# Row maxima of two long attentions taken in parts of 512 keys, rows made by VectorE transposes, a third score bank and values four steps late

## The reference

```python
def gqa_attend(q, k, v):
    s = jnp.einsum('bqhgd,bkhd->bhgqk', q, k).astype(jnp.float32) * (GQA_HEAD_DIM ** -0.5)
    p = jax.nn.softmax(s, axis=-1).astype(v.dtype)
    return jnp.einsum('bhgqk,bkhd->bqhgd', p, v)

def mla_attend(q_nope, q_rope, k_nope, k_rope, v):
    s = (jnp.einsum('bqhd,bkhd->bhqk', q_nope, k_nope)
         + jnp.einsum('bqhr,bkr->bhqk', q_rope, k_rope)).astype(jnp.float32) * ((MLA_NOPE + MLA_ROPE) ** -0.5)
    p = jax.nn.softmax(s, axis=-1).astype(v.dtype)
    return jnp.einsum('bhqk,bkhd->bqhd', p, v)
```

## Time and profile before

| | us |
|---|---|
| median of 3 runs | 3588.08 (3584.24 to 3592.72) |
| the profiled execution's own time | 3586.85 |
| its span, first to last instruction | 3585.0 |
| PE busy in the span | 3351.6 (93%) |
| DVE, ACT, POOL busy | 2186.5 (61%), 1793.4 (50%), 1535.2 (43%) |
| GQA attention, first maxima to the end of its values | about 1819.6 to 2381 |
| MLA attention, the same | about 2917.9 to 3487 |

### The profile page before, as it was taken

The page is one execution under the profiler, slowest core; times in us unless marked ns, Lnnn a source line. Parts: engine busy times, 40 slices in busy tenths (PEclk is TensorE's granted clock), DMA queues, the critical chain, the costliest instruction groups (busy, mean ns, idle before and its releaser), DMA issues.

```text
span 3585.0 us, 47856 instructions
## 1 busy us (share of the span) xinstructions
PE 3351.6 (93%) x14934; PEld 2655.1 (74%) x14934; DVE 2186.5 (61%) x2655; ACT 1793.4 (50%) x3060; POOL 1535.2 (43%) x977
## 2 busy tenths in 40 slices
PE   7999999999999999799889999989888989999999
PEld 5777877778888887587777777767765667777767
DVE  6674877477575757447246666666558865555551
ACT  3343868242010101434158888861465657887870
POOL 3303444434444444510156666656210026666652
PEclk9999999999999999899999999999999989999999
DMA  2134232311212121123433443412254344332311
GB/s 99 53 117 119 75 77 81 119 41 66 75 59 88 55 86 35 58 102 115 124 89 66 102 85 76 103 64 89 97 197 149 118 118 111 65 82 53 76 42 71
DMA packets 196086, 313.52 MB, mean 87 GB/s; under 512 B 100928, under 2 KB 111680, under 8 KB 195968
## 3 DMA queue, kind: packets, MB, share of 16 engines
q1 hardware_dynamic: 195968, 312.01, 29.8%
HBM read 234.02 MB, written 77.92 MB: 87 GB/s over the span
## 4 chain that ended last, share of the span: by engine, by line
PE 68%; DVE 12%; issue 7%; ACT 6%; POOL 3%; DMA 2%; SPq 2%; DVEq 0%; ACTq 0%; POOLq 0%
PE PBX L281 10%; PE PBX L283 10%; PE PBX L282 10%; PE PMX L281 5%; PE PMX L282 5%; PE PMX L283 5%; PE PMX L1952 4%; PE PD L1993 2%; PE PD L1994 2%; PE PD L1995 2%; PE PD L856 2%; DVE gqa_m L2083 1%; PE PBX L1977 1%; PE PBX L1976 1%; PE PBX L1978 1%
## 5 line engine op out<-in xcount | busy, mean ns | idle before, releaser
L216 POOL TENSOR_TENSOR w_hi<-w_stage,zero 128x1024 fp32r<-128x1024 f32 (+2 forms) x123 | 229.1, 1863 | 1263.4 <-PE PBX L283 789.3
L2061 POOL TENSOR_TENSOR gqa_pl<-gqa_pf,gqa_ph 128x512 fp32r<-128x512 f32 (+1 forms) x288 | 370.9, 1305 | 186.3 <-ACT gqa_ph L2034 185.7
L2061 POOL TENSOR_TENSOR mla_pl<-mla_pf,mla_ph 128x512 fp32r<-128x512 f32 x256 | 351.8, 1383 | 206.9 <-ACT mla_ph L2034 202.7
L2083 DVE TENSOR_REDUCE gqa_m<-PMX 128x1 f32<-128x1280 f32 (+1 forms) x158 | 200.9, 1271 | 173.6 <-PE PMX L1952 172.7
L218 POOL TENSOR_TENSOR w_lo<-w_stage,w_hi 128x1024 fp32r<-128x1024 f32 (+2 forms) x123 | 299.9, 2438 | 9.7
L1678 ACT ACTIVATE conv_in<-PBX 128x512 f32<-128x512 f32 x66 | 39.6, 601 | 480.6 <-PE PBX L283 476.6
L2083 DVE TENSOR_REDUCE mla_m<-PMX 128x1 f32<-128x1280 f32 x126 | 187.3, 1487 | 89.5 <-PE PMX L1952 88.9
L2029 ACT ACTIVATE mla_pf<-PBX 128x512 f32<-128x512 f32 x320 | 190.1, 594 | 98.0 <-PE PBX L1978 88.1
L2029 ACT ACTIVATE gqa_pf<-PBX 128x512 f32<-128x512 f32 (+1 forms) x352 | 202.1, 574 | 52.8 <-PE PBX L1981 48.6
L2034 ACT ACTIVATE gqa_ph<-gqa_pf 128x512 fp32r<-128x512 f32 (+1 forms) x352 | 215.6, 612 | 13.8
L281 PE MATMUL PBX<-ffn_hi,w_hi 128*128 128x512 f32 x528 | 207.5, 393 | 8.5 <-DVE ffn_lo L653 8.5
(11 more groups left out here) (411 smaller groups left out, 9915.1 us busy)
## 6 DMA issues: line engine op xcount, KB each, us to landing
mod_w<-in_w_mod SPq DMA_DIRECT2D x48, 512.0 KB, 3.5
w_stage<-in_w_up SPq DMA_DIRECT2D x44, 512.0 KB, 3.4
w_stage<-in_w_go SPq DMA_DIRECT2D x24, 512.0 KB, 3.8
gqa_k<-kh_d SPq DMA_DIRECT2D x32, 320.0 KB, 4.9
gqa_q<-qh_d SPq DMA_DIRECT2D x32, 320.0 KB, 7.7
w_stage<-in_w_down SPq DMA_DIRECT2D x24, 384.0 KB, 3.0
qh_d<-heads_qh SPq DMA_DIRECT2D x32, 256.0 KB, 2.0
ql_d<-heads_ql SPq DMA_DIRECT2D x32, 256.0 KB, 2.3
```

The costliest lines, as they stand in the source:

```text
L216: pool.tensor_tensor(w_hi[s][:, 0:st.cols], w_stage[s][:, 0:st.cols], z, ALU.add).then_inc(w_hi_done, 1)
L2061: eng.tensor_tensor(self.PL[k % 4][:, 0:n], self.PF[k % 4][:, 0:n], self.PH[k % 4][:, 0:n].bitcast(F32), ALU.subtract).then_inc(self.lo_dv ...
L2083: dve.tensor_reduce(self.M[g % 2][:, t:t + 1], MX[:, 0:w], AX.X, ALU.max, negate=True)\
```

## The change

- Maxima are taken in **parts** of 512, 512 and 256 keys (`part_keys`): each part is one matmul and one reduction, and goes to one of two banks of PMX in turn. The parts of a tile are spread over two steps.
- The row is made on DVE alone (`row`): a small reduction over the parts with the sign turned, four 32-partition transposes and a copy. `diag`, `bcast` and ACT's `row` are gone.
- Scores have 3 banks in GQA and 4 in MLA, and `PF`, `PH`, `PL` rings of 6 and 5 in place of 4. `O` has a bank for each chunk.
- `LAG` is 4 in place of 3 for PE and ACT, and `LAG + 2` for DVE's `final`.
- The two half-width steps of the context chunk are one step, so a GQA head has 21 steps.
- The plan: the coming head's first maxima stand at step 11 (GQA; 12 before) and 10 (MLA, as before), and its second chunk's first tile is taken in the same head too.

```diff
-            LAG = 3
+            LAG = 4
...
-                self.S = [PB[0], PB[1]]
-                self.BC = PB[2]
-                self.O = [PD[0], PD[1]]
+                self.S = [PB[0], PB[1], PB[2]] + [PMX[:, 2 * C:3 * C]] * self.mla
+                self.NS, self.NP = len(self.S), len(self.PF)
+                self.O = [PD[0], PD[1], PMX[:, 2 * C:3 * C]][:len(chunks)]
+                self.MX = [PMX[:, 0:C], PMX[:, C:2 * C]]
...
-                    plan = [(2 * t, "max", (0, 1), t) for t in range(4)] + [(8, "bcast", (0, 1), 0)]
-                    plan += [(8 + 2 * t, "max", (0, 2), t) for t in range(2)] + [(12, "bcast", (0, 2), 0)]
-                    plan += [(12 + 2 * t, "max", (1, 0), t) for t in range(4)] + [(21, "bcast", (1, 0), 0)]
+                    plan = [u for t in range(1, 4) for u in tile((2 * t - 2, 2 * t - 1, 2 * t - 1), (0, 1), t)]
+                    plan += [(7 + t, (0, 2), t, 0) for t in range(2)]
+                    plan += [u for t in range(4) for u in tile((11 + 2 * t, 12 + 2 * t, 12 + 2 * t), (1, 0), t)]
+                    plan += tile((19, 20, 20), (1, 1), 0)
...
-                        sp.wait_ge(self.pv, i * self.SB + (CR_PV2 + self.SB // 2))
+                        sp.wait_ge(self.pv, i * self.SB + (self.NP + self.SB // 2))
...
-                    pe.wait_ge(self.exp, i * SB + (k - 2 + CR_E + 1))
+                    pe.wait_ge(self.exp, i * SB + (k + 1))
...
+                    for b in range(4):
+                        dve.transpose(blocks[:, :, b, :], NEG[32 * b:32 * b + 32, 0:m, :]).then_inc(self.turned, 1)
...
-                self.run(dve, step, lambda i, k: final(i, k) if self.steps[k][4] else None)
+                self.run(dve, step, lambda i, k: final(i, k) if self.steps[k][4] else None, lag=self.LAG + 2)
```

More of the change, by code:

```diff
@@ L1779, in mixed_program, with __init__ @@
         class Attention:
-            LAG = 3
-            def __init__(self, name, scope, chunks, keys, scale, layout, mix, first):
+            LAG = 4
+            def __init__(self, name, scope, chunks, keys, scale, layout, mix, first, ring):
                 self.name, self.chunks, self.keys, self.scale, self.mix = name, chunks, keys, scale, mix
@@ L1821, in __init__, with tile @@
+                self.steps = [(q, c, g, x == 0, x == len(self.groups[c]) - 1) for q in range(2)
+                              for c in range(len(chunks)) for x, g in enumerate(self.groups[c])]
                 self.SB = len(self.steps)
                 self.NC = len(chunks)
+                def tile(steps, at, t):
+                    return [(steps[p], at, t, p) for p in range(3)]
                 if self.mla:
-                    plan = [(2 * t, "max", (0, 1), t) for t in range(4)] + [(8, "bcast", (0, 1), 0)]
@@ new lines, in __init__ @@
+                    plan += [u for t in range(4) for u in tile((10 + 2 * t, 11 + 2 * t, 11 + 2 * t), (1, 0), t)]
+                    plan += tile((18, 19, 19), (1, 1), 0)
+                else:
+                    plan = [u for t in range(1, 4) for u in tile((2 * t - 2, 2 * t - 1, 2 * t - 1), (0, 1), t)]
+                    plan += [(7 + t, (0, 2), t, 0) for t in range(2)]
+                    plan += [u for t in range(4) for u in tile((11 + 2 * t, 12 + 2 * t, 12 + 2 * t), (1, 0), t)]
+                    plan += tile((19, 20, 20), (1, 1), 0)
@@ L1833, in __init__ @@
                 self.plan = plan
-                self.NT = sum(1 for p in plan if p[1] == "max")
+                self.NU = len(plan)
+                self.FIRST = 15
                 self.dve_lo = lambda k: k % (self.SB // 2) % 10 in (3, 8)
@@ L1937, in pe, with maxima @@
                 mr = self.dim if self.mla else P
-                def maxima(i, q, c, t, tile, first_of_head, head, MX=PMX, free=CR_R):
-                    if first_of_head and q == 1:
+                def maxima(i, q, c, t, part, unit, new_head, head, MX=self.MX):
+                    if new_head and q == 1:
                         pe.wait_ge(self.const[1], self.const_n)
-                    if first_of_head:
+                    if new_head:
                         pe.wait_ge(self.loaded[q], head * self.load_inc + self.load_inc)
-                    pe.wait_ge(self.red, i * (2 * self.NT) + (tile + free))
+                    if unit >= len(MX):
+                        pe.wait_ge(self.red, i * (2 * self.NU) + (unit - len(MX) + 1))
@@ L1947, in maxima @@
                     o = self.chunks[c][0] + t * P
[L1948 to L1962, removed]
+                    lo, hi = self.part_keys(c, part)
@@ L1964, in scores @@
+                    pe.matmul(MX[unit % len(MX)][:, 0:hi - lo], self.Q[q][0][0:mr, o:o + P], self.K[q][0][0:mr, lo:hi],
+                              start=True, stop=True).then_inc(self.max, 1)
                 def scores(i, k):
-                    q, c, t, first, _ = self.steps[k]
+                    q, c, tiles, first, _ = self.steps[k]
                     o, n = self.chunks[c]
                     if first:
-                        pe.wait_ge(self.row_done, i * (2 * NC) + (q * NC + c + CR_ROW2 + 1))
@@ L1982, in scores @@
                     mm.then_inc(self.scores, 1)
                 def values(i, k):
-                    q, c, t, first, last_ = self.steps[k]
+                    q, c, tiles, first, last_ = self.steps[k]
                     n = self.chunks[c][1]
```

204 lines of the change are left out of this document (100 added, 104 removed).

## The result

| | before | after |
|---|---|---|
| median of the runs, us | 3586.35 (3584.24 to 3592.72, 4 runs) | 3734.04 (3731.45 to 3736.69, 4 runs) |
| ratio | | 1.0409, 95% interval 1.0391 to 1.0427 |
| span of the profiled execution, us | 3585.0 | 3733.4 |
| mean granted clock in it | 0.977 | 0.956 |
| time from one head's load to the next, GQA / MLA, us | 34.4 / 34.5 | 40.6 / 39.3 |

The account below looks back on a forecast made before the run. PE was taken as the bound, stopping for each next head's load after the change. GQA +60, MLA +50, first and last heads -8 and starts +4 made +106 us: 3692 us, range 3605 to 3750.

Parts of the forecast that it names:

- The load: Next head's reload: 15.1 us release to use in GQA, 11.8 in MLA, against 9.0 of PE work; stops 6.1 and 2.8.
- Rival C: Next head's load lands in time, so the change only gains what it removes: 3499 us; chance 0.13.
- The clock: PE's granted clock drops after each load stop, costing 2.5 us per GQA stop and 2.2 per MLA stop.
- Rival B: PE stops for loads, but the clock holds or comes back inside the stop: 3626 us; chance 0.17.
- my own premise: Stops of 2.8 or 6.1 us exceed the 1.03 us wait that lowered PE's clock, so it falls after each.
- What remains is local: PE's remaining wait for DVE, at step 18's row: 0.7 us per GQA head, 0.3 per MLA head (0 to 2).
- DVE's work: DVE's operations per GQA head total 28 us, below PE's 29.4.
- rival D: DVE becomes the bound because transposes take 1.49 us, making a row 6.7 us: 3842 us; chance 0.04.
- The one wait that I looked at: Step 20's last part waits on DVE, whose row precedes step 19's reduction: 3.5 us against PE's 2.8 in GQA.
- The sum: Per head: release to use, remaining PE work (20.4 GQA, 23.7 MLA), DVE wait and clock; 38.7 and 38.0 us.
- Rival C's price: Time if loads were in time: 3499 us, with -69 us in GQA and -23 in MLA over 16 heads each.

Follow-up runs that it names:

- Experiments 1: Changed kernel without reloads: each of the two sets of K, Q and V loaded once per attention; 3607.7 us, 1.006 of the kernel before.
- experiment 4: Changed kernel with each head's load split, the K and Q tiles the maxima read going first with their own semaphore; 3610.2 us, ratio 1.0068 to before.
- experiment 5: Kernel before with both buffer releases one step later, nothing else changed; 3644.5 us, ratio 1.0153.
- experiment 2: Changed kernel with thrown-away matmuls ahead of the wait for the load, 21 in GQA and 11 in MLA; 3680.5 us, ratio 1.0265 to before.
- experiments 4 and 9: The second of the two: changed kernel with four maxima banks in GQA, loads not split; 3693.5 us, ratio 1.0297 to before.
- experiment 7: Changed kernel with split loads and, in GQA, four maxima banks, two score banks and two output banks; 3539.8 us, ratio 0.9864 to before.

## Why the prediction was right, and where it was short

**The load.** Right, and it carries the result: the loads are 126 of the 148 us. Release to use was put at 15.1 and 11.8 us and is 14.8 in GQA; in MLA the last values start at 3140.25, the next matmul at 3140.48, and the maxima that wait at 3152.31, which is 11.8; PE's program up to the need was put at 9.0 us, so stops of 6.1 and 2.8 us. Measured are 5.1 and 3.0. In GQA 0.3 us of the difference is the shorter load and about 0.6 a wait for DVE inside the nine us (2121.79), which the stop swallowed. Experiments 1, 4 and 5 show the cause from three sides: no reload, only the first tiles waited for, and the kernel before with a later release. Rival C, the load in time, is out. In GQA one of the two lost steps comes from the lag and one from the plan, whose maxima stand at step 11; no run takes back the second alone.

**The clock.** Right in kind and near in size. I took 2.5 us per GQA stop and 2.2 per MLA stop, and filling the stop gave back 2.8 and 2.1. The granted clock of the steady parts gives (1 - 0.91) x 528 / 13 = 3.7 and (1 - 0.95) x 471 / 12 = 2.0; this counts lowered clock also where PE stood still and lost nothing by it, so I go by the filled stops. Rival B, the clock unharmed, is out. By the rule of the Trainium skill ("TensorE: Matmul & The Clock Gate", "Why this matters for your kernels") the MLA stops, put at 2.8 us, would have been spared. Measurement and rule differ here: the twelve MLA stops were 2.50 to 3.36 us long, and ten of them brought the clock down, that of 2.50 us too. But my own premise, that a stop longer than the 1.03 us of the earlier trace rows brings it down every time, fails as well: behind the stops of 2.80 and 3.00 us the clock stayed at full. Two of the stops:

```profile
3152.31 0.79 PE L1964 MATMUL PMX<-mla_k,mla_q 96*128 96x512 f32 x1 [2.73 <-DMA mla_q<-ql_d]
3152.90 0.63 PE L1980 MATMUL PBX<-mla_q,mla_k 97*128 97x512 f32 x1
...
3269.38 0.49 PE L1964 MATMUL PMX<-mla_k,mla_q 96*128 96x512 f32 x1 [3.00 <-DMA mla_q<-ql_d]
3269.71 0.40 PE L1980 MATMUL PBX<-mla_q,mla_k 97*128 97x512 f32 x1
```

So the length of a stop alone does not tell whether the clock falls. In GQA it fell to 0.50 behind all thirteen (4.66 to 5.55 us). Nor do the short waits tell more: with the stops filled (experiment 2) thirteen waits of 0.93 to 1.05 us left it at 1.00, while in after it fell behind one of 0.96 us (2149.75).

**DVE.** This is the step that failed: "What remains is local ... I add 0.7 us per GQA head and 0.3 per MLA head". Measured are 26.9 / 13 = 2.1 and 13.1 / 12 = 1.1 us on PE, and 4.5 a head in GQA once the stop no longer hides part of it (experiment 4). DVE's work was right, 365.5 / 13 = 28.1 us a head where I had 28, and so were nearly all the durations in it:

```profile
L2072 DVE TENSOR_REDUCE gqa_m<-PMX 128x1 f32<-128x512 f32 x252 | 173.5, 689 | 158.5 <-PE PMX L1964 157.5
...
L2050 DVE TENSOR_TENSOR gqa_pl<-gqa_pf,gqa_ph 128x512 fp32r<-128x512 f32 x64 | 62.4, 975 | 21.1 <-ACT gqa_ph L2030 20.0
L2088 DVE STREAM_TRANSPOSE gqa_row<-gqa_neg 32x128 f32<-32x128 f32 x128 | 38.8, 303 | 5.3
```

A transpose takes 0.303 us, as taken, and a reduction of 512 keys 0.69, as before. So rival D, slow transposes, is out. (The low half took 0.975 us where I had 0.83; see the last section.) The one wait that I looked at is there, at the last part of step 20, and was put at 0.7. What I missed are the others, one head of after:

```profile
2149.75 0.38 PE L1964 MATMUL PMX<-gqa_k,gqa_q 128*128 128x256 f32 x1 [0.96 <-DVE gqa_m L2072]
2151.80 0.69 PE L1964 MATMUL PMX<-gqa_k,gqa_q 128*128 128x512 f32 x1 [0.42 <-DVE gqa_m L2072]
2164.11 0.39 PE L1964 MATMUL PMX<-gqa_k,gqa_q 128*128 128x256 f32 x1 [0.59 <-DVE gqa_m L2072]
```

They are those of steps 20, 0 and 7. I looked at the row of step 18 without the low half behind it (L2050, 1.41 us from 2149.73), which the part of step 0 waits for, and at none of steps 4 to 9, where two rows, the finals and two low halves follow each other on DVE without a gap. A queue of two parts is used up before DVE returns.

**The sum.** GQA: 14.8 + 20.4 + 2.1 + 2.8 = 40.1 against 40.6 measured and 38.7 forecast. About 0.5 of the 2.1 lies inside the 14.8, and the waits are shown some 0.17 us short each, 46 of them in 13 heads, which is 0.6 us a head the other way; 0.4 us a head I can't place. MLA: 11.8 + 23.7 + 1.1 + 2.1 = 38.7 against 39.3 measured and 38.0 forecast; some 0.2 of the missing 0.6 are waits shown too short (17 in 12 heads), the rest I can't place. Against the forecast that is 1.9 x 14 + 1.3 x 14 = 45 us, and 42 were missing; 1.4 and 0.8 us a head, or 31 us, are the waits for DVE.

**Rival C's price.** It was wrong for the same reason. With the load out of the way the time is 3608 to 3610, not 3499. The 110 us can be won, but behind a second limit: four banks and less work on DVE bring the kernel to 3488. Had the load been in time, I should have forecast a gain where there is a loss of 22 to 24 us. So the right direction rests on the load alone.

## What to carry to other kernels

A longer lag between producer and consumer also postpones the release of every buffer that the consumer reads: one step later cost the kernel before 57 us (experiment 5). Count release to use of the next prefetch before adding a step, and where the first consumer reads one tile of a set, give that tile a semaphore of its own. An engine that is 64% busy can still stop another: look at its longest unbroken run in program order, and compare that with the depth of the queue in front of it. Two limits can stand one behind the other at the same line, so that lifting either alone shows too little: the split alone and the banks alone both left the kernel slower than before (experiments 4 and 9), and together they made it 1.4% faster (experiment 7).

## What the runs showed of the hardware that was new to me

- A stop of 4.9 us cost another 3.1 us behind it, through 6.5 us at 0.52 of the clock in which PE was busy all the time. A stop of 3.00 us in MLA cost no clock, one of 2.73 did. Thrown-away matmuls in the stop kept it at 1.00 and made the kernel 53 us faster.
- Some DVE operations took longer than the same form elsewhere. The copy of a row took 0.664 us in GQA and 1.083 in MLA. The gate multiply, which took 0.687 us in GQA, took 1.219 in MLA, and 0.686 in the kernel before, where its first input is another tile:

```profile
L2090 DVE CAST mla_q<-mla_row 1x512 fp32r<-1x512 f32 x32 | 34.6, 1083 | 1.1
L2103 DVE TENSOR_TENSOR MIX<-MIX,mla_gate 64x512 f32 x28 | 34.1, 1219 | 1.7
L2090 DVE CAST gqa_q<-gqa_row 1x512 fp32r<-1x512 f32 x32 | 21.3, 664 | 1.1
```

The low half on DVE went from 829 ns to 975 in GQA. No run was made on the cause, so it stays open. POOL is a suspect: in experiment 4 the low half on DVE took 0.69 us at 2161.62, while POOL stood idle, and 1.65 at 2171.02, while POOL made low halves. But a copy of a row took 0.42 us at 2166.26 with POOL at work beside it.
